# Eighteen matmuls on a tile of zeros ahead of the first chunk of a two-block transformer kernel

## The reference

```python
u = rmsnorm(h, g_mix_pre[i])          # h = x at the start
proj = u @ w_in[i]                    # 256 x 2048 by 2048 x 12288
qa, ka, va, qb, kb, vb, ga, gb = jnp.split(proj, split_points, axis=-1)
```

## Time and profile before

| what | us |
|---|---|
| median of 3 runs | 2672.47 |
| lowest and highest | 2670.52 and 2673.8 |
| profiled execution | 2669.47 |
| its span | 2667.7 |
| TensorE busy | 2633.3 (99%) |
| VectorE busy | 1757.2 (66%) |
| ScalarE busy | 1210.8 (45%) |
| start of the first matmul in the span | 8.11 |

### The profile page before, as it was taken

One profiled execution on the slowest core, in us unless ns is written; L12 is line 12 of the kernel. 1 busy time (PEld: TensorE's weight loads), 2 busy tenths in 40 slices (PEclk: granted clock), 3 DMA queues, 4 the chain that ended last, 5 costly groups with the idle time before them and its releaser, 6 DMA issues. The chain is left out here.

```text
span 2667.7 us, 34007 instructions
## 1 busy us (share of the span) xinstructions
PE 2633.3 (99%) x12084; PEld 2179.9 (82%) x12084; DVE 1757.2 (66%) x1870; ACT 1210.8 (45%) x1548; POOL 42.6 (2%) x71
## 2 busy tenths in 40 slices
PE   8999999999999999999999999999999999999998
PEld 7888888887888888788888888888888888888887
DVE  5656555456766666666676687777777777746655
ACT  5544544444644444444446443443443344444544
POOL 0000000000000000000000100000000000000000
PEclk9999999999999999999999899999999999899999
DMA  7455555556677777777766387777777776354344
GB/s 252 163 174 173 174 196 197 189 191 197 228 257 258 262 257 260 259 260 260 260 231 205 127 282 255 243 256 243 255 249 253 259 246 204 121 189 154 106 135 157
DMA packets 286709, 575.93 MB, mean 216 GB/s; under 512 B 13842, under 2 KB 53394, under 8 KB 286098
## 3 DMA queue, kind: packets, MB, share of 16 engines
q1 hardware_dynamic: 255376, 466.65, 53.5%
q10 hardware_dynamic: 31236, 107.94, 11.2%
HBM read 572.45 MB, written 2.10 MB: 215 GB/s over the span
## 5 line engine op out<-in xcount | busy, mean ns | idle before, releaser
L1586 DVE TENSOR_TENSOR lo<-raw,hi 128x1024 fp32r<-128x1024 f32 (+1 forms) x890 | 1078.0, 1217 | 743.0 <-ACT hi L1051 741.1
L1051 ACT ACTIVATE hi<-raw 128x1024 fp32r<-128x1024 f32 (+1 forms) x890 | 935.8, 1055 | 1217.1 <-PE panels L508 1077.8
L506 PE MATMUL panels<-hi,xT_hi 128*128 128x512 f32 x2224 | 879.3, 395 | 9.0 <-DVE lo L1586 9.0
L508 PE MATMUL panels<-hi,xT_lo 128*128 128x512 f32 x2224 | 869.4, 391 | 0.0
L507 PE MATMUL panels<-lo,xT_hi 128*128 128x512 f32 x2224 | 868.6, 391 | 0.0
L506 PEld LDWEIGHTS panels<-hi,xT_hi 128*128 128x128 f32 x2224 | 419.8, 189 | 94.9 <-issue 9.0
L508 PEld LDWEIGHTS panels<-hi,xT_lo 128*128 128x128 f32 x2224 | 419.3, 189 | 88.8
L507 PEld LDWEIGHTS panels<-lo,xT_hi 128*128 128x128 f32 x2224 | 419.8, 189 | 85.1 <-issue 0.2
L506 PE MATMUL panels<-hi,yT_hi 128*128 128x512 f32 (+1 forms) x1024 | 399.9, 391 | 5.4 <-issue 4.3
L508 PE MATMUL panels<-hi,yT_lo 128*128 128x512 f32 (+1 forms) x1024 | 395.5, 386 | 0.0
L507 PE MATMUL panels<-lo,yT_hi 128*128 128x512 f32 (+1 forms) x1024 | 395.2, 386 | 0.0
(11 more groups left out here) (210 smaller groups left out, 1311.3 us busy)
## 6 DMA issues: line engine op xcount, KB each, us to landing
work<-ada_w ACTq DMA_DIRECT2D x192, 512.0 KB, 4.5
raw<-w_in SPq DMA_DIRECT2D x79, 1024.0 KB
raw<-w_up SPq DMA_DIRECT2D x64, 1024.0 KB
raw<-w_down SPq DMA_DIRECT2D x64, 1024.0 KB
raw<-ret_w_in SPq DMA_DIRECT2D x64, 1024.0 KB
raw<-ret_w_in SPq DMA_DIRECT2D x64, 512.0 KB
raw<-ret_w_out SPq DMA_DIRECT2D x32, 1024.0 KB
raw<-mla_w_in SPq DMA_DIRECT2D x24, 1024.0 KB
```

What stands on the lines that cost most here:

```text
L506: pe.matmul(o, x_hi[:, kt0 + j, ms], w_hi, start=first and j == 0, stop=False)
L508: done = pe.matmul(o, x_lo[:, kt0 + j, ms], w_hi, start=False, stop=last and j == kts - 1)
L1051: act.activation(hi[:, k % HI_CHUNKS, 0:words], raw[:, slot, k % 2 * CHUNK:k % 2 * CHUNK + words], copy).then_inc(hi_ready, 1)
L1586: dve.tensor_tensor(lo[:, k % HI_CHUNKS, 0:words], raw[:, k // 2 % RAW_SLOTS, k % 2 * CHUNK:k % 2 * CHUNK + words], hi[:, k % HI_CHUNKS, 0 ...
```

## The change

VectorE sets 512 columns of `row` to zero and copies them into `yT_lo[0]`, which has the type of the matmuls' operands. TensorE waits for both and then runs eighteen matmuls of 128x512 on this tile into `score[1]`, ahead of chunk 0. Their result is used by nobody.

```diff
+WARM_MATMULS = 18
...
+        zeros, warm = row[:, 0:N], yT_lo[0][:, 0:2, :].rearrange("p a t -> p (a t)")
...
-        ones_set = sem("ones_set")
+        ones_set, warm_set = sem("ones_set"), sem("warm_set")
...
+            pe.wait_ge(warm_set, 2)
+            for _ in range(WARM_MATMULS):
+                pe.matmul(score[1], warm[:, 0:P], warm, start=True, stop=True)
 
             for s in range(8):
                 if s < 2:
...
         @block.vector
         def _(dve):
             t = Tally(dve)
+            dve.memset(zeros, 0.0).then_inc(warm_set, 1)
+            dve.wait_ge(warm_set, 1)
+            dve.tensor_copy(warm, zeros).then_inc(warm_set, 1)
```

## The result

| | before | changed |
|---|---|---|
| median of 17 runs, us | 2670.45 | 2675.62 |
| lowest to highest | 2667.98 to 2674.84 | 2671.6 to 2678.09 |
| profiled execution, its span | 2669.47, 2667.7 | 2671.6, 2669.5 |

The ratio of changed to before is 1.0017, with a 95% interval of 1.001 to 1.0023: the change makes the kernel slower by about 4.5 us (5.2 us by the medians). It had been forecast 0.95 us faster. 2675.62 lies above the range, although the median of before came out 2.0 us lower in 17 runs than in the three that the forecast started from. 0.0017 is inside the 0.2%, at its slower end; the interval reaches a little beyond it.

What follows compares the result with a forecast made beforehand. TensorE bounds the kernel, busy 2633.3 of 2667.7 us. Chunk 2 starting at 16.78 instead of 17.73 gains 0.95 us, which takes the median from 2672.47 to 2671.5 us; range 2668.8 to 2674.9.

Steps and rivals of the forecast that it cites:

- the 0.2%: Whole kernel: 5.3 us, about what a measurement can't tell from no change; chance of staying within it 0.95.
- The start: TensorE up to chunk 2: dummies raise the clock, chunk 0 runs at 2.4 GHz, chunk 2 starts 0.95 us earlier.
- the wait for lo_norm(2): TensorE before turn_input(4), ahead of chunk 2: a new wait of about 0.9 us on VectorE's lo_norm(2).
- the 4.12 us wait: TensorE's idle stretch before 666.74 us: its first matmul behind was to come at about 665.8.
- that rival: Dummies at the start don't lift the clock, because they hold zeros or come too late: 2674.4 us; chance 0.09.
- Every later chunk is one us earlier than it was: All work behind chunk 2: the gain at the start persists, later waits shifting with TensorE's own last matmul.
- The sum: Whole kernel: span 2667.7 - 0.95 = 2666.75 us; the same gain on the median 2672.47 gives 2671.5.
- The last sign: TensorE's waits that end by "issue": the forecast would be wrong if they changed by more than the gain.
- The program moves in its memory: TensorE's three waits ending by "issue", 4.3 us together: thirty-six more instructions change them 2 us either way; chance 0.08.
- The chances by size: Whole kernel against 2672.47 us: within 0.2% 0.95, faster 0.03, slower 0.02.
- costed cases: Whole-kernel times worked out for the forecast and its rivals, all within 0.2% of 2672.47 us.
- the rival of the falling clock: TensorE's wait ahead of turn_input(4): the clock falls again, 2.1 to 2.8 us given back, 2674.0 us; chance 0.05.

## Why the prediction was wrong, point by point

- *The start* was right, in mechanism and, in the first profile, nearly in size; in the second, late weights left 0.13 us of the 0.95, since the prediction took its loads from one profile. Forecast and measured in the first: dummies from 2.1, 1.91 us; the two operations of VectorE 0.5 and 0.68, measured 0.48 and 0.43; chunk 0 from 9.0, 8.80; the change of spacing between the tenth and fifteenth dummy, behind the fourteenth; the wait for lo_norm(2) about 0.9, 1.24; chunk 2 at 16.78, 16.93; the end of the 4.12 us wait at 665.8, 665.97. Zeros lift the clock as other operands do, so that rival is out, and the clock didn't fall in the wait ahead of turn_input(4).
- *"Every later chunk is one us earlier than it was"* is the step that failed. Chunk 2 is 0.80 us earlier, the work at 666 us 0.77 and that at 941 us 0.39; behind the loop the kernel is 5.75 us later. The sum put at nothing what the head of the feed-forward loop pays for fetching instructions, which changes with its place in the program. Measured in its place: 4.2 us more of pauses and 1.5 us of low clock. The last sign that the prediction named for being wrong is the one that came, waits that end by "issue" changing by more than the gain.
- *The program moves in its memory* was the rival that came true, with a chance of 0.08 and 2 us either way. Its place and its direction could not be read from the trace of before, but its size could have been bounded better: in that trace the two longest of the three waits stand behind a jump back, so each round pays again, and a second pause behind each would have been 4 us, with a fall of the clock on top. Measured: 4.2 us and 1.5 us. With 6 us either way its upper end, 2671.5 + 6 = 2677.5, would have been outside the range that I gave.
- *The chances by size* held: the slowdown is 0.17%, within the 0.2%. That is partly luck: the chance of 0.95 was reasoned from costed cases, and the loss of 4.5 us is larger than any of them.

## What to carry to other kernels

The place of an instruction in the program can cost or gain more than its work: when a kernel has a long hand-unrolled loop on an engine, look for waits at the heads of its rounds that end at no semaphore, count the packets of the instruction queue, and measure a change ahead of the loop against a control with as many empty instructions. Here the changed kernel with 14 more dummies, or with 32 narrow ones, is 0.3% faster than before; with 32 dummies of 2 columns, which give the loop the same place and leave the clock low, it is 0.23% faster. Such a gain is tied to the place, and the next edit ahead of the loop can lose it. And a gain on an engine that was slow is limited by the wait that comes next: of 2.5 us on chunk 0, 0.80 and 0.13 reached chunk 2 in the two profiles.

## What the runs showed of the hardware that was not expected

- Whether the clock falls behind a pause of 2 us varies. Behind the first pair of the changed kernel it was at half for 3 us in both profiles (0.50 and 0.52 from 950 to 953 us); behind the pair 180 us later, of nearly the same length (2.01 and 1.73; 2.30 and 1.52), it was full in both. Behind the single pause at a head it stayed full in the kernel before (2.09 us), but was 0.50 from 1126 to 1128 us with 36 increments behind the loop (2.10 us), and 0.51 from 1129 to 1131 us with 36 in front (1.99 us). So the 2.1 us on which I rested the rival of the falling clock were no safe bound.
- A semaphore increment on TensorE takes about 0.15 us: from 64 to 150 of them the first matmul moves from 11.80 to 24.92 us, and to 32.67 with 200.
- Dummies of 2 columns, 32 in about 6.9 us, left the clock low; 32 of 256 columns in 6.2 us raised it.
